# Convolution taps as 32x32 diagonal tiles on TensorE, and rotation tables as products of two 16-entry tables

## The reference

```
def conformer_conv(u2, dw_w, dw_b, ln_g, ln_b, pw2_w):
    a, b = jnp.split(u2, 2, axis=-1)
    h = a * jax.nn.sigmoid(b)
    h = conv_general_dilated(h, dw_w, padding=(30, 0), feature_group_count=256) + dw_b   # 31 taps, causal
    h = jax.nn.silu(layer_norm(h, ln_g, ln_b))
    return h @ pw2_w

def s5_ssm(u, lam_re, lam_im, log_dt, b_re, b_im, c_re, c_im, d, glu_w):
    ...
    mag = jnp.exp(lr * dt)
    ar, ai = mag * jnp.cos(li * dt), mag * jnp.sin(li * dt)     # 16 groups x 64 states
    ...                                                         # x[t] = (ar + i ai) x[t-1] + bu[t]
    y = real part of C x, over 256 steps
```

## Time and profile before

| | |
|---|---|
| Median of 3 runs | 1241.56 us (1241.49 to 1247.09) |
| Profiled execution, its own time | 1245.72 us |
| Its span, first to last instruction | 1243.9 us |
| Mean granted TensorE clock | 0.959 of full speed |
| Busy: PE / PEld / DVE / ACT / POOL | 92% / 86% / 62% / 50% / 14% |
| PE's share of the chain that ended last | 74% |

### The profile page before, as it was taken

One profiled execution on the slowest core, in us unless ns is written; L12 is line 12 of the kernel. 1 busy time (PEld: TensorE's weight loads), 2 busy tenths in 40 slices (PEclk: granted clock), 3 DMA queues, 4 the chain that ended last, 5 costly groups with the idle time before them and its releaser, 6 DMA issues.

```text
span 1243.9 us, 21859 instructions
## 1 busy us (share of the span) xinstructions
PE 1144.2 (92%) x8526; PEld 1063.6 (86%) x8526; DVE 772.0 (62%) x1148; ACT 619.9 (50%) x1101; POOL 173.1 (14%) x260
## 2 busy tenths in 40 slices
PE   5987879898999999989988899999988799999997
PEld 4876657798999999989955699999986669999997
DVE  3699884465566566666455375666666657665663
ACT  4643334554455455464454364554554476454553
POOL 2399992010010000010000010000010001000000
PEclk8988788999999999999988899999999899999999
DMA  7424112335266766546430055666675405566650
GB/s 248 142 97 142 62 35 68 102 99 173 68 191 192 202 175 181 163 149 185 130 94 1 1 170 165 173 202 188 183 135 136 102 1 169 154 186 202 178 160 34
DMA packets 218142, 169.05 MB, mean 136 GB/s; under 512 B 20787, under 2 KB 208098, under 8 KB 217954
## 3 DMA queue, kind: packets, MB, share of 16 engines
q1 hardware_dynamic: 216962, 164.44, 45.5%
q0 software_dynamic: 496, 2.43, 0.5%
q10 hardware_dynamic: 624, 1.35, 0.4%
HBM read 167.15 MB, written 1.05 MB: 135 GB/s over the span
## 4 chain that ended last, share of the span: by engine, by line
PE 74%; DVE 15%; ACT 7%; issue 2%; SPq 1%; DMA 1%; POOL 0%; POOLq 0%; ACTq 0%; DVEq 0%
PE bank L1926 20%; PE bank L1928 19%; PE bank L1927 19%; PE bank L1989 11%; DVE wlo L1332 4%; DVE arena L1325 3%; ACT whi L787 2%; DVE arena L1478 1%; DVE arena L1516 1%; PE bank L1983 1%; PE bank L1985 1%; PE bank L1984 1%; ACT arena L1280 1%; SPq L662 1%; DVE hf L1343 1%
## 5 line engine op out<-in xcount | busy, mean ns | idle before, releaser
L1926 PE MATMUL bank<-mem_hi,whi 128*128 128x256 f32 x1408 | 407.5, 289 | 8.0 <-DVE mem_lo L1625 5.8
L1927 PE MATMUL bank<-mem_lo,whi 128*128 128x256 f32 x1408 | 401.0, 285 | 0.0
L1928 PE MATMUL bank<-mem_hi,wlo 128*128 128x256 f32 x1408 | 400.8, 285 | 0.0
L1926 PEld LDWEIGHTS bank<-mem_hi,whi 128*128 128x128 f32 x1408 | 273.0, 194 | 11.6 <-issue 8.7
L1926 PE MATMUL bank<-act_hi,whi 128*128 128x256 f32 (+1 forms) x920 | 265.3, 288 | 12.5 <-DVE act_lo L1351 4.4
L1927 PEld LDWEIGHTS bank<-mem_lo,whi 128*128 128x128 f32 x1408 | 272.9, 194 | 1.9 <-issue 1.7
L1928 PEld LDWEIGHTS bank<-mem_hi,wlo 128*128 128x128 f32 x1408 | 272.7, 194 | 0.0
L1927 PE MATMUL bank<-act_lo,whi 128*128 128x256 f32 (+1 forms) x920 | 261.4, 284 | 0.0
L1928 PE MATMUL bank<-act_hi,wlo 128*128 128x256 f32 (+1 forms) x920 | 261.3, 284 | 0.0
L1332 DVE TENSOR_TENSOR wlo<-raw,whi 128x1024 fp32r<-128x1024 f32 (+3 forms) x137 | 165.0, 1247 | 109.3 <-ACT whi L787 107.7
L1700 DVE TENSOR_TENSOR wlo<-raw,whi 128x1024 fp32r<-128x1024 f32 x177 | 208.8, 1220 | 3.9
(11 more groups left out here) (211 smaller groups left out, 1195.5 us busy)
## 6 DMA issues: line engine op xcount, KB each, us to landing
raw<-in_ffn_w_in_dram SPq DMA_DIRECT2D x132, 512.0 KB, 5.2
raw<-in_ffn_w_out_dram SPq DMA_DIRECT2D x33, 1024.0 KB, 5.0
raw<-in_w_in_ab_dram SPq DMA_DIRECT2D x11, 1024.0 KB, 5.3
raw<-in_w_in_dram SPq DMA_DIRECT2D x9, 1024.0 KB, 6.9
raw<-in_xa_wk_dram SPq DMA_DIRECT2D x4, 1024.0 KB, 5.7
raw<-in_xa_wv_dram SPq DMA_DIRECT2D x4, 1024.0 KB, 5.1
raw<-in_w_out_dram SPq DMA_DIRECT2D x4, 1024.0 KB, 5.1
raw<-in_xa_wq_dram SPq DMA_DIRECT2D x4, 1024.0 KB, 5.1
```

The source lines that it names most:

```text
L1926: pe.matmul(dst, w[0], a[0], start=start, stop=False, **kw)
L1927: pe.matmul(dst, w[0], a[1], start=False, stop=False, **kw)
L1928: return pe.matmul(dst, w[1], a[0], start=False, stop=stop, **kw)
```

## The change

1. The taps go to PE. DVE multiplies a 32x32 identity by each channel's tap weight into `conv_diag` (two products of 128x992: 31 taps x 32 columns for each half), right behind `conv_in`. `conv_taps(c)` on PE then runs 31 x 4 matmuls with a 32x32 diagonal as weights and 256 columns of `conv_in`: half 0 behind k2, half 1 behind k3. Even taps write row block i to partitions of block i in bank 7, odd taps row block i to block i+1 in bank 6. ACT copies bank 6 out (`conv_part_out`), PE adds it back shifted by a matmul with a rolled identity (`conv_sum`, 128x512), and ACT adds the bias (`conv_out`). All taps on DVE and POOL go.
2. The rotation tables. DVE reduces the angle and 16 times the angle, multiplies both by 0 to 15 and reduces again (`reduce`, `phase`, 128x256); ACT takes two more sines of 128x256; DVE turns one into a cosine. POOL then forms each half of the tables with six products, sums and differences of 128x1024, in place of the doubling. The small tables lie in `bu`, so `bu_out(0)` on ACT waits for both halves.
3. `inputs_of(1)` and `bu_out(1)` move from behind k3 to behind v0 on PE and ACT, since bank 6 is taken by the taps. The constants grow by 176 columns of the early table.

The diff, cut to its core:

```
@@ gpsimd: rotation tables
             pool.wait_ge(s_coef, 3)
             for half, rot_ in enumerate((rot_early, rot_late)):
                 states = slice(4 * half, 4 * half + 4)
-                ... (eight rounds of doubling, 13 instructions for most)
+                ones_c, ones_s = (x[:, 0, states, :].unsqueeze(2).to_broadcast([P, 4, 16, 16]) for x in (turn_cos, turn_sin))
+                tens_c, tens_s = (x[:, 1, states, :].unsqueeze(3).to_broadcast([P, 4, 16, 16]) for x in (turn_cos, turn_sin))
+                mul(c, tens_c, ones_c)
+                step(mul(tmp, tens_s, ones_s))
+                step(pool.tensor_tensor(c, c, tmp, ALU.subtract))
+                mul(s_, tens_s, ones_c)
+                step(mul(tmp, tens_c, ones_s))
+                pool.tensor_tensor(s_, s_, tmp, ALU.add).then_inc(s_rotr, 1)
                 pool.wait_ge(s_rotr, half + 1)
-            pool.wait_ge(s_conv_in, 2)
-            for j in range(SHARED_TAPS, 31):
-                step(pool.tensor_scalar(tap_product, conv_in[:, 1, j:j + T], w, None, ALU.mult))
-                ins_ = pool.tensor_tensor(conv_y[:, 1, :], tap_product, conv_y[:, 1, :], ALU.add)
@@ scalar
             act.activation(half_sin, angle, ACT.Sin, scale=0.5).then_inc(s_angle, 1)
+            act.activation(turn_sin, phase, ACT.Sin).then_inc(s_angle, 1)
+            act.activation(turn_cos, phase, ACT.Sin, scale=0.5).then_inc(s_angle, 1)
@@ scalar: bu_out
                 act.wait_ge(s_bu, s + 1)
+                if s == 0:
+                    act.wait_ge(s_rotr, 2)
@@ scalar: order
-            for j in range(4):
-                qk_squares(j)
-                if j == 3:
-                    bu_out(0)
-                    bu_out(1)
+            qk_squares(0) ... qk_squares(3)
+            bu_out(0)
             for i in range(4):
                 evacuate("v", i, v_sb[:, i % 2, T * (i // 2):T * (i // 2) + T])
                 if i == 0:
                     rms_of(("qk", 3), bank[4][:], 64, 512)
+                    conv_part_out()
+                    bu_out(1)
+                    conv_out()
@@ vector: angles
+            reduce(t0, turns)
+            dve.tensor_scalar(angle, t0, BOUND, -BOUND, ALU.min, ALU.max)
+            step(dve.tensor_scalar(t1, t0, 16.0, None, ALU.mult))
+            reduce(t1, turns)
+            for w, x in enumerate((t0, t1)):
+                step(mul(phase[:, w], x.unsqueeze(2).to_broadcast([P, 8, 16]), steps16))
+            reduce(phase, phase_tmp)
+            dve.tensor_scalar(phase, phase, BOUND, -BOUND, ALU.min, ALU.max).then_inc(s_coef, 1)
...
-            dve.wait_ge(s_angle, 4)
+            dve.wait_ge(s_angle, 6)
+            step(mul(turn_cos, turn_cos, turn_cos))
+            dve.tensor_scalar(turn_cos, turn_cos, -2.0, 1.0, ALU.mult, ALU.add)
@@ vector: behind conv_in
             mul(conv_in[:, :, 30:30 + T], conv_y, gate).then_inc(s_conv_in, 1)
+            for c in range(2):
+                mul(conv_diag[:, c, :, :], w.unsqueeze(2).to_broadcast([P, TAPS, 32]),
+                    ident32.unsqueeze(1).to_broadcast([P, TAPS, 32])).then_inc(s_diag, 1)
...
-                    convolve(1, 0, SHARED_TAPS, s_conv_in)
-                if 1 <= j < 3:
-                    convolve(0, 10 * j - 10, 10 * j)
...
-            convolve(0, 20, 31, s_conv)
@@ tensor
+            def conv_taps(c):
+                pe.wait_ge(s_conv_in, 1)
+                pe.wait_ge(s_diag, c + 1)
+                pe.wait_ge(s_bc_ev, 2)
+                for j in range(TAPS):
+                    s = j % 2
+                    b = conv_banks[s][:, c * T:c * T + T]          # (bank[7], bank[6])
+                    for i in range(4):
+                        r, to = slice(32 * i, 32 * i + 32), 32 * ((i + s) % 4)
+                        last = plain(b[to:to + 32, :], conv_diag[r, c, j, :], conv_in[r, c, j:j + T], ...)
+                last.then_inc(s_cv, 1)
+            def conv_sum():
+                pe.wait_ge(s_cvp, 1)
+                plain(conv_banks[0][:], ident2[:, 32:32 + P], conv_part, False, True).then_inc(s_cvs, 1)
             for j in range(4):
                 project("k", j, ("w_in", "k", j // 2), P * (j % 2))
+                if j >= 2:
+                    conv_taps(j - 2)
                 if j == 3:
                     inputs_of(0)
-                    inputs_of(1)
             for i in range(4):
                 project_tokens("v", i, ("w_in", "v", i // 2), i % 2)
                 if i == 0:
                     sum_squares(("qk", 3), 0, bank[4][:], 2, True, True, blocks)
+                    inputs_of(1)
+                    conv_sum()
```

More of the change, by code:

```diff
@@ L55 @@
 DILATIONS = (1, 4, 16)
[L56 removed]
+TAPS = 31
 SOFTMAX_FILL = 14
@@ L234, in constant_table @@
     cols.append(("ident", np.eye(P)))
+    cols.append(("again", np.eye(P)))
+    cols.append(("ident32", np.tile(np.eye(32), (4, 1))))
     blocks = np.zeros((P, P)); blocks[:64, :64] = 1; blocks[64:, 64:] = 1
@@ L241, in constant_table @@
     cols.append(("seen", np.where(k[:, None] < k[None, :], 0.0, -1e30)))
+    cols.append(("steps", np.tile(np.arange(16.0), (P, 1))))
     cols.append(("even_group", np.stack([1 - (k // 16) % 2, (k // 16) % 2], 1)))
@@ L535, in bu_bank @@
         def bu_bank(s):
-            return {0: 7, 1: 6}.get(s, 4)
+            return {0: 5, 1: 6}.get(s, 4)
+        conv_banks = (bank[7], bank[6])
         def lat_flat(a, b):
@@ L954, in qk_squares, with conv_part_out, conv_out @@
                         after(n, j)
-            for j in range(4):
-                qk_squares(j)
-                if j == 3:
-                    bu_out(0)
-                    bu_out(1)
+            def conv_part_out():
+                act.wait_ge(s_cv, 2)
+                act.activation(conv_part, conv_banks[1][:], ACT.Copy).then_inc(s_cvp, 1)
+            def conv_out():
+                act.wait_ge(s_cvs, 1)
+                for c in range(2):
+                    b_ = ROW["conv_dw_b"] + c
+                    last = act.activation(conv_y[:, c, :], conv_banks[0][:, c * T:c * T + T], ACT.Identity, bias=col[:, b_:b_ + 1])
+                last.then_inc(s_cvy, 1)
+            qk_squares(0)
+            qk_squares(1)
+            qk_squares(2)
+            qk_squares(3)
+            bu_out(0)
             for i in range(4):
@@ L1459, in _ @@
             mul(conv_in[:, :, 30:30 + T], conv_y, gate).then_inc(s_conv_in, 1)
-            dve.wait_ge(s_conv_in, 1)
+            for c in range(2):
+                w = tap[:].rearrange("p (j c) -> p c j", c=2)[:, c, :]
+                mul(conv_diag[:, c, :, :], w.unsqueeze(2).to_broadcast([P, TAPS, 32]),
+                    ident32.unsqueeze(1).to_broadcast([P, TAPS, 32])).then_inc(s_diag, 1)
             def qk_norm(j):
@@ L1467, in qk_norm @@
                         .then_inc(ev["dve"], 1)
-            def convolve(c, first, last, done=None):
-                for j in range(first, last):
-                    w = tap[:, 2 * j + c:2 * j + c + 1]
-                    src = conv_in[:, c, j:j + T]
-                    if j == 0:
-                        b = ROW["conv_dw_b"] + c
-                        ins_ = dve.tensor_scalar(conv_y[:, c, :], src, w, col[:, b:b + 1], ALU.mult, ALU.add)
-                    else:
-                        ins_ = dve.scalar_tensor_tensor(conv_y[:, c, :], src, w, conv_y[:, c, :], ALU.mult, ALU.add)
-                    if j == last - 1 and done is not None:
-                        ins_.then_inc(done, 1)
-                    else:
-                        step(ins_)
             for j in range(4):
```

76 lines of the change are left out of this document (31 added, 45 removed).

## The result

| | time, us | span of the profiled execution, us | granted clock |
|---|---|---|---|
| before (beside the change) | 1243.63, median of 4 (1241.49 to 1247.09) | 1243.9 | 0.959 |
| changed | 1269.25, median of 4 (1267.91 to 1269.81) | 1267.9 | 0.958 |

The ratio is 1.0204 with a 95% interval of 1.0168 to 1.0239: the change makes the kernel 2% slower. The forecast was 1261 us in a range of 1238 to 1275 us.

A forecast was written before the change was run, and what follows sets the result against it. Between 50 and 250 us PE waits for DVE, which is slow where POOL is busy. Terms of 27.3 + 7.6 + 5.1 − 20.4 = +19.6 us gave 1265 us for the profile, 1261 us for the median, range 1238 to 1275.

The forecast's parts named there:

- Part 1: New angle work on DVE and ACT before POOL's tables: 4.35 us, so POOL starts at 54.1 us.
- Part 2: POOL's twelve table operations: 24.7 us plus 3.7 between, ending at 82.5 us, one small DVE operation behind each.
- Part 3: DVE's remaining work from POOL's end to q2: 9.8 us, q2 at 92.4 instead of 65.09 us, +27.3 us.
- Part 4: q2 to the end of v3: two waits go, taps of 16 us and half clock come, together +7.6 us.
- Part 5: v3 to quarter 1: `sums_of(0)` comes later behind a split and quarter 0, half clock again, +5.1 us.
- Part 6: State quarters 1 to 3: with POOL idle each takes 10.1 us, 48.6 instead of 69.0 us, −20.4 us.
- Behind the stretch: Behind 195.1 us: PE is its own bound and nothing changes.
- Slower taps: Rival on PE's taps: dense issue fails or only four tiles run together, 26.7 us, 1266 to 1274 us; chance 0.17.
- one tile at a time: Rival on PE's taps: row tiles cannot share a PSUM bank, 106.6 us of taps, 1352 us; chance 0.05.
- Blocking in part: Rival on DVE beside POOL: several or small operations pass, half of 21.4 us saved, 1245 to 1257 us; chance 0.12.
- no blocking: Rival on DVE between 54 and 82 us: POOL hardly holds it, q2 at 71.0 us, 1238 us; chance 0.11.
- The one on the other side: The rival of no blocking, not slower: −3.3 us, 1238 us, or 1235.7 with taps at 13.4; chance 0.11.

The follow-up runs named there:

- kernel 3: Changed kernel, but POOL starts the table products only after DVE's coefficient chain and the diagonals; 1253.9 us, ratio 1.0076.
- kernel 4: Changed kernel with each of POOL's 12 table operations of 128x1024 cut into four of 128x256; 1257.16 us, ratio 1.0105.
- Kernel 7: Kernel 6 with the first state quarter on DVE ahead of the splits behind v0 and v1; 1238.24 us (0.9948), repeated 1237.72 us (0.9954).
- kernel 5: Changed kernel with odd taps not turned to the next 32 output rows, so four tiles serve both banks; 1282.58 us, ratio 1.0314.
- Kernel 6: As kernel 3, but POOL waits for DVE's copies of the state matrices and the small tables lie in the keys' buffer; 1247.08 us, ratio 1.0025.
- kernel 2: Changed kernel with only the taps on PE, the tables by doubling on POOL as before; 1244.45 us, ratio 0.9998.
- kernel 9: kernel 2 with the first state quarter ahead of the splits behind v0 and v1, doubling still on POOL; 1237.55 us, ratio 0.9952.
- kernel 1: Changed kernel with only the new rotation tables, the convolution on DVE and POOL as before; 1259.1 us, ratio 1.0113.

## Why the prediction was right, and where its sum was off

The direction and the mechanism held: POOL's long operations hold DVE's chain, q2 comes late, and the quarters give less than that back. The sum was +19.6 us, the span grew by 24.0.

- *Part 1, tables ahead.* POOL was to start at 54.1 us and started at 55.76. DVE's stretch began 2.3 us later than before (39.18 us, 36.92 before). At least 1.4 us of that are not the change: kernel 3 has the same code up to there and began at 37.82. The added work itself took 3.7 us against my 4.35 with ACT's.
- *Part 2, twelve operations.* Forecast 28.4 us from start to end, measured 28.3; a pair takes 3.83 us, 1.92 each against my 2.06. That the sum agrees so well is luck in part: 23.0 us are the operations and 5.3 what comes between, where I had 24.7 and 3.7. A small DVE operation that waits pays the whole of one POOL operation, but not every one waits: 15 got through in the time of nine POOL operations, where I had one for each. By the Trainium skill (SBUF — State Buffer, "SBUF: two separate sides"), where the holder of the shared ports keeps them for its whole instruction, this is what must be seen; the rows of 128x8 at 1.85 us and kernel 4 agree.
- *Part 3, q2.* Forecast +27.3 us, measured +26.8, and here too errors cancel. DVE's stretch began 2.3 us later, which the sum did not have. From POOL's end to q2 it took 7.8 us instead of 9.8, since DVE had all its small operations and most of a split behind it by then. Against kernel 3, and counted from the start of DVE's stretch, the blocking is 19.9 us where I had 21.4: 16.0 on the 15 small operations (19.0 instead of 3.05), 1.7 and 2.1 on the two pairs of splits.
- *Part 4, q2 to v3's end.* Forecast +7.6 us, measured +9.4 (91.89 to 142.08 us). The taps were cheaper than taken (14.2 instead of 16). The term that was mis-sized is the half clock. Behind q2's wait it cost what I took, but it comes a second time behind the wait of 1.92 us for the copy of the parts: the granted clock is 0.83 over the 10 us from 130 us, which is 3.4 us at 0.50 (+1.7). A wait of 0.78 us ahead of the first taps was not in the sum either. The last 1.1 us (9.4 − 7.6 + 1.8 − 1.7 − 0.8) I can't place.
- *Part 5, v3 to quarter 1.* Forecast +5.1, measured +5.5 us. Kernel 7 shows that it was the order on DVE alone: one line moved took the wait away.
- *Part 6, the quarters.* Forecast −20.4, measured −18.7 us: each is 10.1 us and two turns 16.5 and 16.7 as said, but the last quarter with its outputs took 17.1 us, where my 48.6 us left 13.8 to 15.2 for it: the clock fell once more (0.83 over the 20 us from 190 us, 6.8 us at 0.50), and PE was busy with its own work until 213.2 us, 2 us after the quarter was done.
- Behind the stretch +1.0 us, forecast nothing. Together 26.8 + 9.4 + 5.5 − 18.7 + 1.0 = 24.0.
- The other 3.8 us of the 8.2 by which 1261 fell short of 1269.25 are the offset between profile and median: I carried 4.2 us over, and the changed kernel's profiled execution lay 0.4 us above its median.

*The rivals.* "Slower taps" and "one tile at a time" fell with the 7.11 us; that rule of the Trainium skill (TensorEngine Tiling (Array Packing), Restrictions and Gotchas), by which different row tiles cannot be at one bank at once, does not hold for this kernel. With one row group at a bank at a time, the taps' two banks would let two matmuls run at once; kernel 5, with four row groups in each bank, has 3.9 and the changed kernel 7.5. "Blocking in part" and "no blocking" fell with the rows of 1.85 us. The one on the other side was priced too low: I had put it at −3.3 us. Kernel 6, where nothing that PE waits for is blocked, comes nearest to it and has +3.1 (0.25%, −0.02 to +0.53%). 4.9 us of the difference are what parts 4 to 6 and the end of the kernel came out higher, which would make it +1.6.

What the prediction did not ask is what each part is worth alone. The quarters gain as much with the taps alone (33.3 us between the scans of 1 and 3, kernel 2) as with both. Once the taps are off POOL, the product tables shorten its stretch from 84 us (50.5 to 134.5, kernel 9) to 28 and buy nothing, as nobody waits for its end.

## What to carry to other kernels

An engine that shares its way to memory should be costed by the length of its longest single operation, not by its total: gathering GpSimd's work from many short operations into twelve long ones made VectorE's critical chain 20 us longer. Before two savings are put together, try each alone, since both may save the same wait; and when work leaves an engine, look again at the order of what stays, for here one moved line (kernel 7 against 6) was worth 0.7%.

## What the runs showed of the hardware that was not expected

- A VectorE scaling with a single tensor operand (128x8, `TENSOR_SCALAR`, 0.17 us before) is held by a GpSimd operation as one with two is: 2.02 us at 68.39 us of the changed kernel, and 2.02 us in kernel 1 as well. I had counted only those with two.
- A VectorE product of 128x1024 takes 1.18 to 1.23 us, the same on GpSimd 1.92 us; cut in four, GpSimd takes 0.60 us a piece, 2.4 us together.
- Four splits of 128x1024 on VectorE, 4.62 us alone, took 11.35 to 11.54 us beside GpSimd's products: a wait of 1.7 us for each.
- The start of the stretch on VectorE moved between 36.9 and 39.3 us from one profiled execution to another, also where the code up to there was the same. A difference of 2 us in one profile says nothing.
